# One pipeline over token tiles for normalisation, transposition and latent projection

## The reference, cut to what matters

```python
xn = rms_norm(x, g_pre)                       # rows of 1024
qa, ka, va, za, cq, ckv_raw, kpe_raw, zb, ma, mb = _split_in(xn @ w_in)
cq_n  = rms_norm(cq, g_q)                     # 256 columns, goes on to the q heads
c_kv  = rms_norm(ckv_raw, g_kv)               # 128 columns, an output
k_pe  = _apply_rope(kpe_raw, cos, sin)        # 32 columns, an output
```

## Time and profile before

| | us |
|---|---|
| median of 3 runs (lowest, highest) | 4474.52 (4471.94, 4477.66) |
| span of the profiled execution, first to last instruction | 4485.9 |
| PE busy in that span | 3613.9 (81%) |
| DVE, ACT, POOL busy | 1323.0, 943.0, 366.5 |

### The profile page before, as it was taken

How to read it: one execution, slowest core, us unless ns; L and a number is a source line. 1 busy time by engine, 2 the same in 40 slices (tenths; PEclk the granted TensorE clock), 3 DMA queues, 4 the chain that set the end, 5 groups by cost and what they waited for, 6 DMA issues and landing times. The chain is left out here.

```text
span 4485.9 us, 57605 instructions
## 1 busy us (share of the span) xinstructions
PE 3613.9 (81%) x19368; PEld 3042.1 (68%) x19368; DVE 1323.0 (29%) x3598; ACT 943.0 (21%) x1830; POOL 366.5 (8%) x470
## 2 busy tenths in 40 slices
PE   4899999999888979999899999972444478517989
PEld 3777777787777868888766777751444477416967
DVE  4122222222211121000055555541212122384333
ACT  4322222222211221111134444430000111001021
POOL 0000000000000000000000000002222333102300
PEclk7899999999888879999999999995555556558999
DMA  3233223332222221212110000015553222365534
GB/s 103 96 102 102 95 93 116 106 96 89 80 87 83 75 71 57 71 57 69 70 20 11 12 12 12 12 32 177 190 189 101 68 54 60 122 228 183 182 118 124
DMA packets 312510, 406.73 MB, mean 91 GB/s; under 512 B 74665, under 2 KB 272010, under 8 KB 307034
## 3 DMA queue, kind: packets, MB, share of 16 engines
q1 hardware_dynamic: 278154, 249.11, 18.4%
q0 software_dynamic: 24976, 151.29, 9.6%
q10 hardware_dynamic: 9216, 4.20, 0.3%
HBM read 317.28 MB, written 175.28 MB: 110 GB/s over the span
## 5 line engine op out<-in xcount | busy, mean ns | idle before, releaser
L109 PE MATMUL dil_S<-all_xT_hi,dil_w_hi 128*128 128x512 f32 x1152 | 465.6, 404 | 17.9 <-DVE dil_w_lo L621 17.9
L111 PE MATMUL dil_S<-all_xT_hi,dil_w_lo 128*128 128x512 f32 x1152 | 456.8, 397 | 0.0
L110 PE MATMUL dil_S<-all_xT_lo,dil_w_hi 128*128 128x512 f32 x1152 | 456.4, 396 | 0.0
L109 PE MATMUL gate_ps<-all_xT_hi,gate_w_hi 128*128 128x512 f32 x768 | 306.6, 399 | 10.3 <-DVE gate_w_lo L891 10.3
L111 PE MATMUL gate_ps<-all_xT_hi,gate_w_lo 128*128 128x512 f32 x768 | 305.0, 397 | 0.0
L110 PE MATMUL gate_ps<-all_xT_lo,gate_w_hi 128*128 128x512 f32 x768 | 304.0, 396 | 0.0
L1173 PE MATMUL mla_S<-mla_k,mla_q 96*128 96x512 f32 (+3 forms) x640 | 285.6, 564 | 15.0 <-ACT mla_p L1060 8.4
L1201 PE MATMUL mla_O<-mla_v,mla_pT 128*128 128x66 f32 x2176 | 265.2, 271 | 2.6 <-DVE mla_pT L1120 1.7
L109 PEld LDWEIGHTS dil_S<-all_xT_hi,dil_w_hi 128*128 128x128 f32 x1152 | 222.3, 193 | 62.1 <-DVE dil_w_lo L621 18.0
L1201 PEld LDWEIGHTS mla_O<-mla_v,mla_pT 128*128 128x128 f32 x2176 | 258.7, 192 | 5.0 <-DVE mla_pT L1120 2.6
L111 PEld LDWEIGHTS dil_S<-all_xT_hi,dil_w_lo 128*128 128x128 f32 x1152 | 221.0, 192 | 48.4
(11 more groups left out here) (276 smaller groups left out, 6325.8 us busy)
## 6 DMA issues: line engine op xcount, KB each, us to landing
out_win_sample<-in_state_win POOLq DMA_DIRECT2D x16, 4088.0 KB, 15.0
sdil_kv<-in_state_win SPq DMA_DIRECT2D x72, 512.0 KB
scr_gates<-gate_out POOLq DMA_DIRECT2D x24, 1040.0 KB, 4.5
sdil_qb<-scr_hs SPq DMA_DIRECT2D x32, 768.0 KB
dil_raw<-in_w_in SPq DMA_DIRECT2D x36, 512.0 KB, 4.2
proj_gm<-scr_gates SPq DMA_DIRECT2D x40, 416.0 KB, 3.3
out_win_sample<-in_state_win POOLq DMA_DIRECT2D x4, 4064.0 KB, 2.3
scr_oa<-dil_rec SPq DMA_DIRECT2D x192, 66.0 KB, 1.6
```

Of the source, the lines that this page charges most:

```text
L109: pe.matmul(out, w[0], x[0], start=first, stop=False)
L110: pe.matmul(out, w[0], x[1], start=False, stop=False)
L111: return pe.matmul(out, w[1], x[0], start=False, stop=last)
```

## The change

The two stages become one, `stage_front`. Its engines go through 21 slots. In slot i the tile i is normalised and transposed, tile i-1 gets its high and low part, tile i-2 is projected, tile i-3 gets its sums of squares and is normalised, and tile i-4 has its latents transposed and copied out. On every engine a slot is one call of `body(i)`, and the order inside it is fixed. The weights' pieces are loaded by POOL's queue rather than SP's, and split in slots 0 and 1. The square's unused result goes into the tile's `xn` buffer. The copy of the projection out of PSUM is gone: DVE reads PSUM, and there are two PSUM buffers for it rather than four. The query gain is applied by DVE along rows. The transposed latents are copied out in two instructions per tile, kept for four tiles in one of two buffers, and stored by three DMAs after tiles 3, 7, 11, 15 and 16. `NT` is 16, `TILES` 17, `PROJECT` 2, `STATS` 3 and `TURN` 4; `rows_of(i)` is 128 or, for the last tile, 32; `each_slot` calls `body` for i from 0 to 20.

```diff
-def stage_latents(nc, t, xT, xs, ident):
-        pj = [m.ps(f"pj{b}", [P, 512]) for b in range(4)]
...
-            def _(sp):
-                for c in range(KC):
-                    waits(sp, w_lo, c - 1)
-                    sp.dma_start(raw[c % 2][:, :], t["w_in"][c * P:(c + 1) * P, C_CQ:C_CQ + LAT])\
-                        .then_inc(w_in[c % 2], 16)
...
+                    waits(sp, xn_ready, i - 1)
+                    src = t["x_prompt"][i * P:(i + 1) * P, :] if i < NT else t["x_sample"]
+                    sp.dma_start(xin[i % 2][0:rows_of(i), :], src).then_inc(x_in[i % 2], 16)
+
+                sp.dma_start(xin[0][:, :], t["x_prompt"][0:P, :]).then_inc(x_in[0], 16)
+                sp.dma_start(g[:, :], t["g_pre"].partition_broadcast(P)).then_inc(g_in, 16)
+                sp.dma_start(ident[:, :], t["ident"]).then_inc(ident_in, 16)
+                load(1)
...
+                sp.dma_start(gq[:, :], t["g_q"].partition_broadcast(P)).then_inc(consts, 16)
...
-                sp.wait_ge(turned, NT + 1)
-                for c in range(QL // P):
-                    sp.dma_start(t["cqT"][c], cqT[:, c, :]).then_inc(stored, 16)
-                sp.dma_start(t["ckvT"], ckvT[:, :]).then_inc(stored, 16)
-                sp.dma_start(t["kpeT"], kpeT[:, :]).then_inc(stored, 16)
-                sp.wait_ge(stored, 64)
...
+                def store_turned(i):
+
+                    q, at = i // 4 % 2, slice(i // 4 * 512, min(i // 4 * 512 + 512, TOK))
+                    width = at.stop - at.start
+                    sp.wait_ge(turned, i + 1)
+                    sp.dma_start(t["cqT"][:, :, at].rearrange("c p n -> p c n"), latT[q][:, 0:2, 0:width])\
+                        .then_inc(lat_stored[q], 16)
+                    sp.dma_start(t["ckvT"][:, at], latT[q][:, 2, 0:width]).then_inc(lat_stored[q], 16)
+                    sp.dma_start(t["kpeT"][:, at], kpeT[q][:, 0:width]).then_inc(lat_stored[q], 16)
+
+                def body(i):
+                    if 2 <= i < TILES:
+                        load(i)
+                    if 0 <= i - STATS < TILES:
+                        store_nat(i - STATS)
+                    if 0 <= i - TURN < TILES and ((i - TURN) % 4 == 3 or i - TURN == NT):
+                        store_turned(i - TURN)
+
+                each_slot(body)
...
+            @block.gpsimd
+            def _(pool):
+                for c in range(KC):
+                    waits(pool, w_lo, c - 1)
+                    pool.dma_start(raw[c % 2][:, :], t["w_in"][c * P:(c + 1) * P, C_CQ:C_CQ + LAT])\
+                        .then_inc(w_in[c % 2], 16)
...
+                def square(i):
+
+                    b, r = i % 2, slice(0, rows_of(i))
+                    act.wait_ge(x_in[b], 16 * (i // 2 + 1))
+                    waits(act, inverted, i - 1)
+                    waits(act, tp_ready, i - 1)
+                    act.activation(xn[b][r, :], xin[b][r, :], ACT.Square, accum_out=stat[b][r, 0:1]).then_inc(squared, 1)
+                    act.wait_ge(squared, i + 1)
+                    act.activation(stat[b][r, 1:2], stat[b][r, 0:1], ACT.Sqrt, bias=eps[r, :], scale=1.0 / D)\
+                        .then_inc(rooted, 1)
...
-                def turned_out(i, rows):
-                    b, at = i % 2, slice(i * P, i * P + rows)
+
+                def high(i):
+
                     act.wait_ge(tp_ready, i + 1)
-                    for c in range(QL // P):
-                        act.activation(cqT[:, c, at], tp[b][:, c, 0:rows], ACT.Copy, scale=gq[:, c:c + 1])
-                    act.activation(ckvT[:, at], tp[b][:, 2, 0:rows], ACT.Copy)
-                    act.activation(kpeT[:, at], tp[b][0:ROPE, 3, 0:rows], ACT.Copy).then_inc(turned, 1)
...
                     act.wait_ge(pj_ready, i + 1)
-                    waits(act, nat_ready, i - 1)
-                    r = slice(0, rows)
-                    act.activation(junk_q[r, :], pj[i % 4][r, 0:QL], ACT.Square,
-                                   accum_out=stat[b][r, 0:1]).then_inc(squared, 1)
-                    act.activation(junk_kv[r, :], pj[i % 4][r, QL:QL + KL], ACT.Square,
-                                   accum_out=stat[b][r, 1:2]).then_inc(squared, 1)
-                    act.activation(lat[b][r, :], pj[i % 4][r, 0:LAT], ACT.Copy).then_inc(copied, 1)
...
-                        turned_out(i - 1, P)
-                turned_out(NT, NS)
+                    waits(act, linverted, i - 1)
+                    act.activation(junk_q[r, :], pj[b][r, 0:QL], ACT.Square, accum_out=lstat[b][r, 0:1])\
...
+                def turned_out(i):
+
+                    q, at = i // 4 % 2, slice(i % 4 * P, i % 4 * P + rows_of(i))
+                    act.wait_ge(ltp_ready, i + 1)
+                    waits(act, lat_stored[q], 48 * (i // 8))
+                    act.activation(latT[q][:, :, at], ltp[i % 2][:, 0:3, 0:rows_of(i)], ACT.Copy)
+                    act.activation(kpeT[q][:, at], ltp[i % 2][0:ROPE, 3, 0:rows_of(i)], ACT.Copy).then_inc(turned, 1)
+
+                def body(i):
+                    if i < TILES:
+                        square(i)
+                    if i < 2:
+                        for c in range(4 * i, 4 * i + 4):
+                            split_weights(c)
+                    if 0 <= i - 1 < TILES:
+                        high(i - 1)
+                    if 0 <= i - STATS < TILES:
+                        latent_stats(i - STATS)
+                    if 0 <= i - TURN < TILES:
+                        turned_out(i - TURN)
+
+                each_slot(body)
...
+                    dve.wait_ge(lrooted, i + 1)
+                    dve.reciprocal(lstat[b][r, 4:6], lstat[b][r, 2:4]).then_inc(linverted, 1)
+                    waits(dve, nat_ready, i)
+                    dve.tensor_tensor(rot[b][r, 0:ROPE], pj[b][r, QL + KL:LAT], cs[r, i, 0, :], ALU.mult)
...
+                    waits(dve, ltp_ready, i - 1)
                     waits(dve, nat_stored[b], 32 * (i // 2))
-                    dve.tensor_scalar(nat[b][r, 0:QL], lat[b][r, 0:QL], stat[b][r, 4:5], None, ALU.mult)
-                    dve.scalar_tensor_tensor(nat[b][r, QL:QL + KL], lat[b][r, QL:QL + KL], stat[b][r, 5:6],
-                                             gkv[r, :], ALU.mult, ALU.mult)
+                    dve.scalar_tensor_tensor(nat[b][r, 0:QL], pj[b][r, 0:QL], lstat[b][r, 4:5], gq[r, :], ALU.mult,
+                                             ALU.mult)
+                    dve.scalar_tensor_tensor(nat[b][r, QL:QL + KL], pj[b][r, QL:QL + KL], lstat[b][r, 5:6], gkv[r, :],
+                                             ALU.mult, ALU.mult)
...
+                def body(i):
+                    if i < TILES:
+                        norm(i)
+                    if i < 2:
+                        for c in range(4 * i, 4 * i + 4):
+                            split_weights(c)
+                    if 0 <= i - 1 < TILES:
+                        low(i - 1)
+                    if 0 <= i - STATS < TILES:
+                        latents(i - STATS)
+
+                each_slot(body)
...
+                    pe.wait_ge(xn_ready, i + 1)
+                    waits(pe, lo_ready, i - 1)
...
+                def project(i):
+
+                    pe.wait_ge(lo_ready, i + 1)
+                    waits(pe, nat_ready, i - 1)
+                    for c in range(KC):
+                        if i == 0:
+                            pe.wait_ge(w_lo, c + 1)
+                        last = split_matmul(pe, pj[i % 2][0:rows_of(i), 0:LAT], [place(h, i)[:, c, :] for h in range(2)],
+                                            [w[h][:, c, :] for h in range(2)], c == 0, c == KC - 1)
+                    last.then_inc(pj_ready, 1)
...
                     pe.wait_ge(nat_ready, i + 1)
                     waits(pe, turned, i - 1)
...
-                    waits(pe, copied, i - 3)
...
-                    if i:
-                        turn(i - 1, P)
-                turn(NT, NS)
...
+                def body(i):
+                    if i < TILES:
+                        turn(i)
+                    if 0 <= i - PROJECT < TILES:
+                        project(i - PROJECT)
+                    if 0 <= i - TURN < TILES:
+                        turn_latents(i - TURN)
+
+                each_slot(body)
...
-        stage_norm(nc, t, xT, xs, ident)
-        stage_latents(nc, t, xT, xs, ident)
+        stage_front(nc, t, xT, xs, ident)
```

More of the change, by code:

```diff
@@ L125, in held, with stage_front @@
         eng.sem_inc(ticks, 1)
[L128 to L135, removed]
+def stage_front(nc, t, xT, xs, ident):
     with ExitStack() as ctx:
-        m = Mem(nc, ctx, "norm")
+        m = Mem(nc, ctx, "front")
         xin = [m.sb(f"xin{b}", [P, D]) for b in range(2)]
         xn = [m.sb(f"xn{b}", [P, D]) for b in range(2)]
-        junk = m.sb("junk", [P, D])
         g = m.sb("g_rows", [P, D])
@@ L241, in stage_latents @@
-def stage_latents(nc, t, xT, xs, ident):
[L243 to L258, removed]
```

(34 more changed lines are left out.)

125 lines of the change are left out of this document (72 added, 53 removed).

## The result

| | before | after |
|---|---|---|
| median of 4 runs (lowest, highest), us | 4473.23 (4468.07, 4477.66) | 4506.02 (4503.77, 4512.30) |
| span of the profiled execution | 4485.9 | 4502.2 |
| end of the changed stages in the profile, us | 195.03 | 229.80 |
| first matmul of the next stage, us | 201.82 | 236.44 |

The changed kernel is slower: ratio 1.0077, 95% interval 1.0064 to 1.0091; the medians differ by 32.8 us. The forecast of 4515 was 9 us too high, inside the range, and the sign was right. The two spans differ by 16.3 only, because the profiled execution of before took 12.7 us more than the median of its runs and that of after 3.8 less; the best single measure is the stage itself: it ends 34.8 us later, and the next stage's first matmul comes 34.6 us later.

What follows compares the result with a forecast made beforehand. PE idle 4.1 us per slot plus 8.1 of work makes 12.2; 43.0 + 12 x 12.2 + 19 + 27.2 = 235.6 against 195.0, 40.6 slower, so 4474.5 + 40.6 = 4515 us; range 4484 to 4540.

Steps and rivals of the forecast that it cites:

- The loop: Between PE slots: last latent transposition, copies, next square and scaling leave PE idle 4.1 us per slot.
- PE's part of the slot: PE's work in each slot: 8.1 us, partly at the lower clock; 6.1 at the higher, 10.5 at the lower.
- The loads as a second loop: SP's tile loads, issued behind stores: 10.7 us a slot, hidden below the slot's 12.2.
- The long slots: Slots 8, 12 and 16, where SP waits for copies before loading: 7, 7 and 5 us extra, 19 in all.
- Rival 3: Not slower: clock stays up, tiles land in time, slot 10.2 us, front 187, 4466.5; chance 0.10.
- The start: Front up to slot 4: first tile, weights and first projection; slot 2 starts at 24.5, slot 4 at 43.0.
- The weights' rounds through POOL's queue: At the start: three more rounds of two weight pieces at 3.7 us each, as before; bounds 3.5 and 4.2.
- The drain: From the last square to the stage's end: 27.2 us, including 2.8 for the final stores.
- The sum: Whole front: 43.0 + 12 x 12.2 + 19 + 27.2 = 235.6 us against 195.0, 40.6 slower.
- the clock stays up: Rival for the slots: PE's pauses are short against its work, loads bind at 10.7, 4490; chance 0.14.
- never comes up: Rival for the slots: each begins with transpositions, clock stays low, slot 14.6 us, 4549; chance 0.10.
- the break-even pace: Front's slots: with 64.6 us for start and drain, it equals the old time at 10.9 us a slot.

Runs made afterwards that it cites:

- e1: Changed kernel with the transposed latents copied out, and their grouped stores issued, one slot later: 4469.71 us against 4472.01 for the kernel before, ratio 0.9991.
- e3: Changed kernel with latents copied out and stored one slot later and each load issued one slot earlier: 4418.13 us against 4472.01 before, ratio 0.9874.
- e4: Changed kernel with loads one slot earlier and 20 unread matmuls in PE's pause: 4466.74 us against 4472.01 before, ratio 0.9983.
- e8: Changed kernel with only the grouped stores issued one slot later: 4493.03 us against 4471.96 for the kernel before, ratio 1.0056.
- e5: e3 with the weight pieces issued on SP's queue instead of POOL's: 4421.21 us against 4479.32 for the kernel before, ratio 0.9867.
- e6: Kernel before with only the transposed latents' stores grouped after every four tiles: 4466.61 us against 4479.32 for the kernel before, ratio 0.9961.

## Why the prediction was right

**The loop** was right in kind and nearly in size. The pause before the transpositions is 3.61 in every ordinary slot (4.1 forecast). From square to PE it is 69.24 - 66.20 = 3.04 (3.2 forecast), and from PE's end to the square 66.20 - 65.62 = 0.58 (0.85): the second copy, L285, starts 0.39 after the first, so the two overlap more than I counted. e1 shows the cause: with the copy moved by one slot and nothing else on ACT, the slot is 1.8 us shorter, and only the loads keep it from more.

**PE's part of the slot** came out at 11.65 - 3.61 = 8.0 against 8.1 (the forecast's own terms, 4.7, 2.8 and 0.5, add up to 8.0). The mix of both clock levels was the right choice between 6.1 and 10.5; e3 has 5.92 at the higher one, e4 shows the price of the lower as 2.0 (8.1 - 6.1 forecast). The forecast's 4.7 us at the lower clock in every slot is a mean only: the granted clock is 0.50 from 58.24 to 61.04, 2.8 us, in one slot, and from 69.24 to 74.47, 5.2 us, in the next, so that ordinary slots of 11.0 to 11.3 and of 12.0 to 12.3 us take turns. The ordinary slot is thus 11.65 instead of 12.2, and over 12 slots the forecast is 6.6 us too long. That is the largest part of the error.

**The loads as a second loop** were hidden as forecast, and bind when the first loop is taken away: 10.7 forecast, 9.84 in e1.

**The long slots** were mis-sized: 16.2 us in all, 19 forecast. The mechanism, SP behind `turned_out`, is shown by e8. I had let the load pay up to 2.6 us for the stores ahead of it; in e8 they cost 0.6 to 0.7 of PE's pause, and hardly anything of the landing. Rival 3, stores beside loads, was right on this point alone.

**The start** came out nearly right, but not by its steps. The timeline of the kernel after has the squares of slots 2, 4 and 16, which part the sum:

```profile
25.82 1.05 ACT L250 ACTIVATE front_xn<-front_xin 128x1024 f32<-128x1024 f32 x1
...
43.91 1.06 ACT L250 ACTIVATE front_xn<-front_xin 128x1024 f32<-128x1024 f32 x1 [5.89 <-DMA front_xin<-in_x_prompt]
...
199.92 1.06 ACT L250 ACTIVATE front_xn<-front_xin 32x1024 f32<-32x1024 f32 x1 [4.42 <-DMA front_xin<-in_x_sample]
```

square(2) was forecast for 24.5, square(4) for 43.0. The weights' rounds through POOL's queue were priced at 11.1 for three, bounds 10.5 to 12.6, and took 15.2. So the upper bound was too low: I had bounded a load in a full start by loads in a stretch in which the DMA engines were at 0.42, while here they are at 0.70. Of the 4.1 us that they were over, most was made good: the first low parts were done half a microsecond earlier, and on ACT the next square stands behind the last high part and not, as I had it, behind the last low part. That the start is only 0.9 us off is luck. The Trainium skill, DMA: Bandwidth & Descriptors, section Latency and other measured facts, spoke against this move with 0.4 us more to the first byte, an estimate of 1.2 us for three rounds. The direction agrees with the runs; the trace has 0.9 a piece and 3.2 for three rounds between e5 and the changed kernel, with the load on the engines changed as well.

**The drain** was mis-sized: from square(16) to the end it is 229.80 - 199.92 = 29.9, forecast 27.2. The failed term is the stores at its end, 2.8 forecast and 5.1 measured from the first issue, 224.71, to 229.80. The timeline of the kernel after, the last copy of tile 15, the first store of each of the last two groups and the next stage's first load:

```profile
222.94 0.25 ACT L285 ACTIVATE front_kpeT<-front_ltp 32x128 f32<-32x128 f32 x1
...
224.71 0.42 SPq L214 DMA_DIRECT2D scr_cqT<-front_latT  x1
...
226.56 0.62 SPq L214 DMA_DIRECT2D scr_cqT<-front_latT  x1
...
229.80 6.98 SPq L498 DMA_DIRECT2D dil_raw<-in_w_in  x3
```

SP waits for the sample's latents, whose store it issues at 223.87, before it comes to the stores of tiles 12 to 15, though these had been copied out by 222.94 + 0.25 = 223.19; so two groups of three stores are issued one behind the other where I had counted one. Of the 11.0 us of final stores, about half is saved, as e6 shows for the kernel before.

**The sum**: 43.9 to the first counted square, 156.0 for 12 slots (12 x 11.65 + 16.2), and 29.9: 229.8, against a forecast of 235.6. The errors have both signs and cancel in part: -6.6 and -2.8 for the slots, +0.9 and +2.7 for start and drain, in all -5.8. That the sum is so near is thus partly luck; the loop and its pace are not. What the sum can't know is the rest of the program: the stage is 34.8 us longer, the medians differ by 32.8.

**The rivals.** That the clock stays up, or never comes up, is excluded by 0.78 from 43 to 195. The third needed a clock that stays up and tiles in time. e4 has both, the clock by force: 9.68 us a slot, a little under the 10.2 of the bare loop, and a time 0.2% below the kernel before, as that case had. Its landing time of 2.1 us was no guide, since it came from the sample's 128 KB: the tiles of 512 KB landed in 3.7 us (median) in the changed kernel. The account behind the break-even pace holds in kind: e1's slots from 4 to 16 take 120.6 us (nine of about 9.84, two of 11.84, and 8.39 for the last), so with 64.6 for start and drain it gives 185, 10 us less than before, and e1's front is 4 us shorter. Start and drain are 70.6 us there, 6 more than that account has, which puts the break-even nearer 10.4 us a slot than 10.9.

## What to carry to other kernels

In a pipeline written as one in-order list per engine, ask of each wait in a slot what stands behind it on that engine: a copy-out at the end of a slot that waits for another engine's last instruction closes a loop through all three if the next slot's first producer stands behind it, and a delay of one slot opens it. Do the same for the queue that issues the loads: a store that waits for this slot's result holds the next slot's load. And take out all such loops before judging such a merge, because the second hides behind the first and the clock returns only when the pauses are gone: here +0.8%, -0.1% (not to be told from none) and +0.2% became -1.3%.

## What the runs showed of the hardware

Added work made the kernel faster: 3.72 us of matmuls that no one reads, in a pause of 3.61, shortened the slot by 2.0 us, because the granted clock stayed at 1.00 instead of 0.79. Shorter pauses were already enough to lose it: in e1 PE stood still for 2.2 us a slot, and the clock was 0.83 on the mean (0.50 from 58 to 60 us, behind a pause of 2.23). And a piece of 208 KB, which landed in 2.5 us from SP's queue in the kernel before, took 3.5 from POOL's at the start of the changed one, with the engines busy for 0.70 rather than 0.42.
